# Retention heads on one Trainium2 core: where the first group of new sample states is multiplied

## The reference, cut to what matters

```python
def ret_chunk(state, qkv):
    q, k, v = ...
    decay = jnp.where(diff >= 0, jnp.exp(lg[:, None, None] * jnp.maximum(diff, 0.0)), 0.0)
    qk = jnp.einsum('bihd,bjhd->bhij', q, k) * decay
    o = jnp.einsum('bhij,bjhe->bihe', qk, v)
    o = o + jnp.einsum('bihd,bhde->bihe', q * xi[None, :, :, None], state)
    new_state = (jnp.exp(lg * L)[None, :, None, None] * state
                 + jnp.einsum('bjhd,bjhe->bhde', k * zeta[None, :, :, None], v))
    return new_state, o

def ret_output(o, g, ret_gn, w_out, dtype):
    y = rmsnorm(o, ret_gn.reshape(RET_HEADS, RET_DV)).reshape(b, s, RET_HEADS * RET_DV)
    return ((jax.nn.silu(g.astype(jnp.float32)) * y) @ w_out).astype(dtype)
```

## Time and profile before

| | us |
|---|---|
| median of 3 runs | 1601.35 (1601.34 to 1602.0) |
| profiled execution | 1601.7 |
| its span, first to last instruction | 1599.9 |
| TensorE busy in the span | 1593.4 |
| VectorE busy | 838.5 |
| ScalarE busy | 614.1 |
| POOL busy | 271.3 |

### The profile page before, as it was taken

How to read it: one execution, slowest core, us unless ns; L and a number is a source line. 1 busy time by engine, 2 the same in 40 slices (tenths; PEclk the granted TensorE clock), 3 DMA queues, 4 the chain that set the end, 5 groups by cost and what they waited for, 6 DMA issues and landing times.

```text
span 1599.9 us, 24216 instructions
## 1 busy us (share of the span) xinstructions
PE 1593.4 (100%) x9196; PEld 1536.2 (96%) x9196; DVE 838.5 (52%) x984; ACT 614.1 (38%) x796; POOL 271.3 (17%) x269
## 2 busy tenths in 40 slices
PE   9999999999999999999999999999999999999998
PEld 9999999999999999999999999898989899999987
DVE  6544444787454443445444444674747485444422
ACT  6333222577443332224333223424243354333322
POOL 0111122540211110221111122302030312111000
PEclk9999999999999999999999999999999999999999
DMA  7444344555344443445444345575665755444332
GB/s 219 121 123 131 101 125 142 173 185 171 106 132 127 118 122 109 127 133 140 123 131 123 109 127 191 185 242 207 214 234 190 249 180 141 123 131 131 117 123 102
DMA packets 322145, 239.08 MB, mean 149 GB/s; under 512 B 8432, under 2 KB 286128, under 8 KB 321968
## 3 DMA queue, kind: packets, MB, share of 16 engines
q1 hardware_dynamic: 321808, 237.91, 48.9%
q10 hardware_dynamic: 288, 0.50, 0.1%
HBM read 216.39 MB, written 20.94 MB: 148 GB/s over the span
## 4 chain that ended last, share of the span: by engine, by line
PE 100%; ACT 0%; issue 0%; POOL 0%; DVE 0%; ACTq 0%; POOLq 0%
PE bank L170 26%; PE bank L171 26%; PE bank L172 26%; PE bank L491 2%; PE bank L490 2%; PE bank L489 2%; PE bank L1934 1%; PE bank L1933 1%; PE bank L1932 1%; PE bank L1146 1%; PE bank L398 1%; PE bank L1970 1%; PE bank L2045 1%; PE bank L2001 1%; PE bank L1960 0%; PE bank L985 0%
## 5 line engine op out<-in xcount | busy, mean ns | idle before, releaser
L147 DVE TENSOR_TENSOR WL<-RAW,WH 128x2048 fp32r<-128x2048 f32 (+3 forms) x190 | 399.0, 2102 | 296.0 <-ACT WH L140 295.3
L140 ACT ACTIVATE WH<-RAW 128x2048 fp32r<-128x2048 f32 (+3 forms) x190 | 328.1, 1729 | 560.6 <-PE bank L172 478.1
L170 PE MATMUL bank<-XH,WH 128*128 128x384 f32 x1368 | 458.3, 335 | 0.0
L172 PE MATMUL bank<-XH,WL 128*128 128x384 f32 x1368 | 457.1, 334 | 0.0
L171 PE MATMUL bank<-XL,WH 128*128 128x384 f32 x1368 | 457.0, 334 | 0.0
L170 PEld LDWEIGHTS bank<-XH,WH 128*128 128x128 f32 x1368 | 256.8, 188 | 3.4 <-issue 3.1
L171 PEld LDWEIGHTS bank<-XL,WH 128*128 128x128 f32 x1368 | 256.8, 188 | 0.2
L172 PEld LDWEIGHTS bank<-XH,WL 128*128 128x128 f32 x1368 | 256.8, 188 | 0.0
L655 POOL TENSOR_TENSOR si<-si,rsb 128x384 f32<-128x384 f32 x88 | 94.7, 1076 | 625.3 <-ACT si L526 591.1
L586 DVE TENSOR_TENSOR au<-bank,si 128x384 f32<-128x384 f32 x86 | 48.0, 558 | 250.0 <-PE bank L172 232.3
L170 PE MATMUL bank<-AH,WH 128*128 128x384 f32 x528 | 176.4, 334 | 0.0
(11 more groups left out here) (316 smaller groups left out, 2022.1 us busy)
## 6 DMA issues: line engine op xcount, KB each, us to landing
RAW<-w_ffn_gate_dram SPq DMA_DIRECT2D x86, 512.0 KB, 4.0
RAW<-w_ffn_up_dram SPq DMA_DIRECT2D x86, 512.0 KB, 5.2
RAW<-w_ret_in_dram SPq DMA_DIRECT2D x48, 512.0 KB, 5.1
RAW<-w_ffn_down_dram SPq DMA_DIRECT2D x48, 384.0 KB, 4.0
st<-state_ret_dram SPq DMA_DIRECT2D x32, 512.0 KB, 7.1
new_state_sample_dram<-st SPq DMA_DIRECT2D x32, 512.0 KB, 6.6
RAW<-w_ffn_down_dram SPq DMA_DIRECT2D x48, 320.0 KB, 3.3
RAW<-w_ffn_down_dram SPq DMA_DIRECT2D x22, 512.0 KB, 4.0
```

Source lines behind the costliest of these rows:

```text
L140: ins = act.activation(dst(WH), src, ACT.Copy)
L147: ins = dve.tensor_tensor(dst(WL), src, dst(WH).bitcast(F32), ALU.subtract)
L170: pe.matmul(ps, wh, xh, start=first, stop=False)
L172: return pe.matmul(ps, wl, xh, start=False, stop=last)
```

## The change

It makes four kinds of edits:

- TensorE: group 0 moves from inside gate 1 to directly behind the products of the old states; group 1 moves from gate 2 into gate 1 (ahead of k = 3), group 2 from behind gate 2 into it (ahead of k = 1). Group 0 gets bank 1 in place of bank 5, so `NEW_BANKS` changes for it, the wait for `r_on` goes to group 1, and gate 1, whose bank is 1, waits until group 0 has been taken (`r_ns` 4).
- Pair values: ScalarE writes the sample values twice, straight into `vp`; `vf` and POOL's three copies go. SP starts the four DMAs of each half as soon as that half is written, and from the second head on it issues all eight ahead of the load of chunk 6 instead of behind it (in the first head also ahead of it).
- ScalarE: the high part of the values is written ahead of that of the scores, and ahead of the weight split.
- VectorE: two key rests come ahead of the scores, two behind; values' rest, then scores' rest, then weight split; update 0 directly behind it; then root steps, gate 0, gate 1, update 1.

```diff
-            NEW_BANKS = (bank[2:6] * 3) + [bank[2], bank[3], bank[4], bank[6], bank[7], bank[1]]
+            NEW_BANKS = [bank[2], bank[3], bank[4], bank[1]] + (bank[2:6] * 2) + [bank[2], bank[3], bank[4], bank[6], bank[7], bank[1]]
...
-                    sp.wait_ge(sem("r_vp"), 3 * h + 3)
                     for odd in range(2):
+                        sp.wait_ge(sem("r_vp"), 2 * h + (odd + 1))
                         for j in range(PAIRS):
...
-                            sp.dma_start(vp[other, odd, :], vf[mine, :]).then_inc(sem("r_vd_in"), 16)
+                            sp.dma_start(vp[other, odd, :], vp[mine, odd, :]).then_inc(sem("r_vd_in"), 16)
...
-                    if q == 6:
+                    if q == 5:
                         pair_values(0)
...
+                    pair_values(h)
                     load_weights(h, 6)
-                    pair_values(h)
                     load_weights(h, 7)
...  (pe_head)
+                def new_states(part):
+                    odd, d = part // D, part % D
+                    if part:
+                        pe.wait_ge(sem("r_ns"), N_NEW * h + PAIRS * part)
+                    if part == 3:
+                        pe.wait_ge(sem("r_z"), E * h + 1)
+                    if part == 1:
+                        pe.wait_ge(sem("r_on"), TT * h + 1)
+                    if part == 0:
+                        pe.wait_ge(sem("r_kl"), 4 * h + 4)
+                        pe.wait_ge(sem("r_al"), 2 * h + 1)
...
+                new_states(0)
                 pe.wait_ge(sem("r_vl"), TT * h + TT)
-                pe.wait_ge(sem("r_al"), 2 * h + 1)
+                pe.wait_ge(sem("r_al"), 2 * h + 2)
...
+                    if n == 1:
+                        pe.wait_ge(sem("r_ns"), N_NEW * h + PAIRS)
...
-                gate(1, 3, lambda: new_states(0))
-                gate(2, 1, lambda: new_states(1))
-                new_states(2)
+                gate(1, 3, lambda: new_states(1))
+                gate(2, 1, lambda: new_states(2))
...  (act_head)
-                            act.activation(vf, ps[:, :], ACT.Copy, scale=rsb[:, T + t:T + t + 1]).then_inc(sem("r_v"), 1)
+                            for odd in range(2):
+                                act.activation(vp[:, odd, :], ps[:, :], ACT.Copy, scale=rsb[:, T + t:T + t + 1]).then_inc(sem("r_vp"), 1)
...
+                act.wait_ge(sem("r_vd_in"), self.PAIRED * h + self.PAIRED)
+                act.activation(vd[:, 0, :, :], vp, ACT.Copy).then_inc(sem("r_ah"), 1)
                 act.wait_ge(sem("r_at"), h + 1)
                 act.activation(ah[:, :], at_, ACT.Copy).then_inc(sem("r_ah"), 1)
                 self.look_act(act, h, 3)
-                act.wait_ge(sem("r_vd_in"), self.PAIRED * h + self.PAIRED)
-                act.activation(vd[:, 0, :, :], vp, ACT.Copy).then_inc(sem("r_ah"), 1)
...  (dve_head)
+                key_rests(0)
                 dve.wait_ge(sem("r_scores"), h + 1)
                 dve.tensor_tensor(at_, self.SCORES[:, :], hc[:, DECAY], ALU.mult).then_inc(sem("r_at"), 1)
...
+                key_rests(2)
                 dve.wait_ge(sem("r_ah"), 2 * h + 1)
+                dve.tensor_tensor(vd[:, 1, :, :], vp, vd[:, 0, :, :].bitcast(F32), ALU.subtract).then_inc(sem("r_al"), 1)
+                dve.wait_ge(sem("r_ah"), 2 * h + 2)
                 dve.tensor_tensor(al[:, :], at_, ah[:, :].bitcast(F32), ALU.subtract).then_inc(sem("r_al"), 1)
                 self.look_dve(dve, h, 3)
...
+                new_states(0)
                 dve.wait_ge(sem("r_sq"), TT * h + TT)
...
-                for e in range(2):
-                    gate(e)
-                    new_states(e)
+                gate(0)
+                gate(1)
+                new_states(1)
                 self.look_dve(dve, h, 4)
...  (pool)
-                    pool.tensor_tensor(vp[:, 0, 0:DEC_SEQ], vf[:, 0:DEC_SEQ], ones[:, 0:DEC_SEQ], ALU.mult).then_inc(sem("r_vp"), 1)
-                    pool.tensor_copy(vp[:, 0, DEC_SEQ:HV], vf[:, DEC_SEQ:HV]).then_inc(sem("r_vp"), 1)
-                    pool.tensor_copy(vp[:, 1, :], vf).then_inc(sem("r_vp"), 1)
```

More of the change, by code:

```diff
@@ L1763, in stream_kernel @@
             rst = sb("rst", [P, 3, 4], F32, r)
-            vf = on[:, TT - 1, :]
             vp = sg[:, :, :].rearrange("p e n -> p (e n)")[:, 0:2 * HV].rearrange("p (o n) -> p o n", o=2)
@@ L1971, in pe_head @@
                                       start=(odd == 0 and d == 0), stop=False)
+                def new_states(part):
[9 more added lines that the diff above has]
+                        pe.wait_ge(sem("r_al"), 2 * h + 1)
+                    for n in range(2):
+                        for j in range(PAIRS):
+                            rows = slice(j * PAIR, (j + 1) * PAIR)
+                            mm = pe.matmul(self.NEW_BANKS[PAIRS * part + j][:, :], kl[rows, 2 + odd, d * P:(d + 1) * P],
+                                           vd[rows, n, odd, :], start=(n == 0), stop=(n == 1))
+                    mm.then_inc(sem("r_new"), 1)
+                new_states(0)
                 pe.wait_ge(sem("r_vl"), TT * h + TT)
-                pe.wait_ge(sem("r_al"), 2 * h + 1)
+                pe.wait_ge(sem("r_al"), 2 * h + 2)
                 def weighted(o, block, t, first, last):
@@ L1984, in pe_head @@
                 weighted(o1, 2, 1, False, True).then_inc(sem("r_o"), 1)
[L1988 to L2003, removed]
                 def gate(n, at_k=None, inside=None):
@@ L2199, in dve_head @@
                     ps = self.V_BANKS[t]
-                    dve.wait_ge(sem("r_v"), (TT + 1) * h + (n + 2))
+                    dve.wait_ge(sem("r_v"), TT * h + (n + 1))
                     dve.scalar_tensor_tensor(vl[:, t, :], ps[:, :], rsb[:, T + t:T + t + 1], vh[:, t, :].bitcast(F32),
@@ L2203, in dve_head, with key_rests, new_states @@
                 dve.wait_ge(sem("r_hc_in"), 16 * h + 16)
+                def key_rests(i0):
+                    dve.wait_ge(sem("r_kh"), 4 * h + i0 + 2)
+                    for i in (i0, i0 + 1):
+                        z = ZETA + min(i, 2)
+                        dve.scalar_tensor_tensor(kl[:, i, :], self.turned_keys()[i], hc[:, z:z + 1], kh[:, i, :].bitcast(F32),
+                                                 ALU.mult, ALU.subtract).then_inc(sem("r_kl"), 1)
+                key_rests(0)
                 dve.wait_ge(sem("r_scores"), h + 1)
                 dve.tensor_tensor(at_, self.SCORES[:, :], hc[:, DECAY], ALU.mult).then_inc(sem("r_at"), 1)
[L2206 to L2210, removed]
+                key_rests(2)
                 dve.wait_ge(sem("r_ah"), 2 * h + 1)
+                dve.tensor_tensor(vd[:, 1, :, :], vp, vd[:, 0, :, :].bitcast(F32), ALU.subtract).then_inc(sem("r_al"), 1)
+                dve.wait_ge(sem("r_ah"), 2 * h + 2)
                 dve.tensor_tensor(al[:, :], at_, ah[:, :].bitcast(F32), ALU.subtract).then_inc(sem("r_al"), 1)
                 self.look_dve(dve, h, 3)
-                dve.wait_ge(sem("r_ah"), 2 * h + 2)
-                dve.tensor_tensor(vd[:, 1, :, :], vp, vd[:, 0, :, :].bitcast(F32), ALU.subtract).then_inc(sem("r_al"), 1)
+                def new_states(part):
+                    odd, d = part // D, part % D
+                    dve.wait_ge(sem("r_new"), (4 + D) * h + (part + 1))
+                    for j in range(PAIRS):
+                        n = PAIRS * part + j
+                        old = st[:, 2 * j + odd, d, :]
+                        dve.scalar_tensor_tensor(old, old, hc[:, G16:G16 + 1], self.NEW_BANKS[n][:, :],
+                                                 ALU.mult, ALU.add).then_inc(sem("r_ns"), 1)
+                new_states(0)
                 dve.wait_ge(sem("r_sq"), TT * h + TT)
@@ L2228, in gate @@
                     dve.tensor_tensor(gt[:, e % 2, :], self.G_BANKS[e][:, 0:T], rsb[:, 0:T], ALU.mult).then_inc(sem("r_gt"), 1)
[L2230 to L2237, removed]
                 def z(e):
@@ L2314, in pool @@
                                                        pairs(rot4[:, d, SEQ:T], odd), pairs(rot4[:, 2 + d, SEQ:T], odd), op)                                        .then_inc(sem("r_qz"), 1)
-                    pool.wait_ge(sem("r_v"), (TT + 1) * h + 1)
-                    pool.tensor_tensor(vp[:, 0, 0:DEC_SEQ], vf[:, 0:DEC_SEQ], ones[:, 0:DEC_SEQ], ALU.mult).then_inc(sem("r_vp"), 1)
-                    pool.tensor_copy(vp[:, 0, DEC_SEQ:HV], vf[:, DEC_SEQ:HV]).then_inc(sem("r_vp"), 1)
-                    pool.tensor_copy(vp[:, 1, :], vf).then_inc(sem("r_vp"), 1)
                 norm_adds_pool(pool, self.s + 1)
```

## The result

The changed kernel is slower. Six runs took 1613.97, 1615.48, 1617.08, 1617.10, 1617.21 and 1622.01 us, median 1617.09, against a median of 1601.83 for six runs of the kernel before: a ratio of 1.0097, 95% interval 1.0086 to 1.0108. That is 15.3 us more. The kernel before spreads over 0.7 us, the changed one over 8, and that spread is part of what is to be explained.

What follows compares the result with a forecast made beforehand. The prediction took TensorE's instruction stream to bound the kernel. A new stall of 2.82 us less 0.15 of gaps gave +2.67 us a head, +10.7 over four: 1601.35 + 10.7 = 1612.0 us, range 1610.3 to 1618.9.

Steps and rivals of the forecast that it cites:

- rival A: TensorE's clock falls to half in the stalls: 1618.8 us with four falls, 1613.7 to 1615.4 with one or two; chance 0.26.
- the likeliest case: The forecast itself: four stalls of TensorE, less the gaps saved, clock held; 1612.0 us, chance 0.60.
- Part 4: In gate 2, TensorE's third group waits for VectorE's update 1, held up behind VectorE's gate 1: 2.82 us a head.
- Parts 1 to 3: Gaps around TensorE's tiled groups from moving the first and third: -0.87 + 0.67 + 0.05 = -0.15 us a head.
- parts 1 and 2 alone: First group leaves gate 1 (-0.87 us) and goes behind the old states' products (+0.67): -0.20 us a head.
- The middle value for the switch between two tiled forms: Switch from old states' products to the first group replaces that to the full array: +0.67 us, bounds 0.54 to 0.77.
- the sum: Stall of 2.82 us less 0.15 of gaps: +2.67 us a head, +10.7 over four heads.
- Part 5: Split values reach TensorE's early first group in time, 0.8 us of slack: cost 0, up to 0.3 a head.
- Rival C: Pair DMAs land late, so the first group waits too: 1 to 2 us a head more, 1616 to 1620 us; chance 0.06.
- it is one event: Argument against the clock falling: only one fall seen, at the trace's end, 2.2 us without a matmul; stall hardly longer.
- they may fall all or none: Clock falls would come in all four heads or in none, since the heads are spaced alike.
- Rival B: VectorE's gate 1 runs before TensorE's ends, so no stall and not slower: 1601.2 us; chance 0.04.

Runs made afterwards that it cites:

- experiment 1: Changed kernel with VectorE doing update 1 ahead of gate 1 instead of behind it; 1601.40 us against 1601.55 for the kernel before, ratio 0.9999.
- experiment 2: Changed kernel with TensorE's third group (group 2) back behind gate 2, VectorE's order as changed; 1601.12 us, ratio 0.9997 to the kernel before.
- experiment 7: Kernel before with only VectorE's order changed, to gate 0, gate 1, update 0, update 1; 1623.73 us, ratio 1.0134 to the kernel before.
- experiment 5: As experiment 2, but pair values again written by ScalarE into vf and copied three times by POOL; 1603.07 us against 1601.53 for the kernel before.
- experiment 6: As experiment 2, but SP again loads weight chunk 6 ahead of the pair DMAs; 1602.03 us, ratio 1.0003 to the kernel before.
- experiment 9: Changed kernel with 14 unread matmuls a head ahead of the third group, where TensorE waits for update 1; 1612.43 us against 1601.42 for the kernel before.
- experiment 3: Changed kernel with the third group (group 2) ahead of k = 4 of gate 2 instead of k = 1; 1606.20 us, ratio 1.0030 to the kernel before.
- k = 2: Changed kernel with the third group (group 2) ahead of k = 2 of gate 2 instead of k = 1; 1610.69 us, ratio 1.0056 to the kernel before.
- k = 0: Changed kernel with the third group (group 2) ahead of k = 0 of gate 2 instead of k = 1; 1625.0 us, ratio 1.0148 to the kernel before.

## Why the prediction was right, and where it was short

The prediction gave 1612.0 us, a range of 1610.3 to 1618.9, and 0.94 for slower. The measured median of 1617.09 lies in the range, but where rival A has it, not where the likeliest case does.

- **Part 4, the stall**: right in mechanism and size. With g for the start of the last matmul of gate 1 (1123.67 here), VectorE's gate 1 came at g + 0.38 (predicted 0.37), update 1 at g + 0.85 (0.84), its end at g + 3.56 (3.56), TensorE's restart at g + 3.62 (3.61); the stall is 2.83 (2.82). Experiments 1, 2 and 7 show its cause from three sides.
- **Parts 1 to 3, the gaps**: -0.15 a head predicted, -0.17 measured in experiment 1; parts 1 and 2 alone, -0.20 predicted and -0.20 measured in experiment 2. The first head of the changed kernel, whose clock held, was 85.67 us long against 82.98 before: +2.69, where the sum said +2.67. The middle value for the switch between two tiled forms held: 3.57 us with a tiled group behind as with a full-array matmul. That fits what the Trainium skill says (TensorEngine Tiling (Array Packing), Key Properties), that changing the mode of tiling drains TensorE: here the change from one tiled mode to another took as long as the change to the full array. What a drain costs by itself no run here shows.
- **Part 5, the values in time**: right; no wait of the first group in the trace. The transfers' landing was even quicker, 2.0 us at the median and 2.3 at most, where 2.5 and 4.1 had been read from before. Experiments 5 and 6 show that the cover was real but thin: either of the two edits taken back costs the first head 0.7 to 1.8 us. Rival C's sort of wait exists, then, but not in the changed kernel.
- **Rival A, the clock**: this is the step that failed, "Forecast 0.60, A 0.26". No run of the changed kernel took the 1612.4 us that experiment 9 gives for a full clock; the nearest was 1613.97. The row for it was in the trace of before, a fall 2.2 us behind the last matmul against a stall of 2.8, and it was given too little weight against "it is one event". One event was indeed too few to tell: at the ends of the other ten traces the clock fell 2.7 us (experiment 1) to 4.9 us (experiment 3) behind the last matmul's end, so the distance isn't fixed, and a stall of 2.8 us sometimes brings a fall. Its price, 1.7 us for a fall, was right for one kind of fall and low for the other: the two of the profiled execution cost 4.9 together (1615.4 less 1610.5, the span of experiment 9), 1.6 for the third head's and 3.3 for the fourth's. That "they may fall all or none" is wrong for this execution: two of four heads.
- **Rival B**: it would have needed VectorE's gate 1 to start before TensorE's gate 1 was over. It started 0.38 us behind the last matmul's start, and the time was not 1601.2.

What stays open is why one wait of 2.75 us brings a fall and the next, as long and in the same place, doesn't: the changed kernel had two in four heads, experiment 7 four. How long the clock then stays low does follow a pattern, shown at the end.

## What to carry to other kernels

On an engine that works in order, moving a piece of work earlier moves every wait behind it too. Read the other engine's order against the new one and ask, for each group that waits, which instruction stands in front of its releaser and what that one is waiting for; here it was the very engine that then had to wait. The cost of a stall on TensorE is not its length alone: at 1.2 us it was that within half a microsecond over four heads, at 2.2 us it sometimes was more, and at 2.75 and 3.3 us it cost up to double. If such a wait can't be removed, work of no use in it can be cheaper than standing still, as it was here with 2.75 us (experiment 9).

## What the runs showed of the hardware

Four waits of TensorE, one a head, in a program that otherwise waits only at its start, by their length (wait in each head, time over the kernel before, heads with a fall of the clock in the profiled execution, distance of the lowest to the highest run):

| wait, us | over before, us | falls in 4 heads | runs spread, us |
|---|---|---|---|
| 0.3 (experiment 9, filled) | 11.0 | 0 | 0.5 |
| 1.2 (k = 4) | 4.65 | 0 | 0.8 |
| 2.2 (k = 2) | 9.2 | 1 | 1.7 |
| 2.75 (the change) | 15.3 | 2 | 8.0 |
| 2.75 (experiment 7) | 22.2 | 4 | 5.1 |
| 3.3 (k = 0) | 23.5 | 4 | 2.7 |

The traces of these kernels hold eleven falls in the retention stage, and they are of two kinds, without an exception:

| the clock fell | falls | low for, us | cost, us |
|---|---|---|---|
| 0.2 to 1.6 us behind TensorE's restart | 5 | 3.4 | 1.55 to 1.6 |
| 0.3 to 1.3 us ahead of it, in the wait | 6 | 6.8 | 2.5 to 3.3 |

The cost is what the head was longer than one with the same wait and no fall (for a fourth head, the rest of the span). So the clock stayed low twice as long where it fell while TensorE still stood as where it fell when TensorE had resumed, and the five late falls slowed work that waited for nothing. Experiment 7 cost more than the changed kernel because three of its four falls were long ones. Why the low time has just these two lengths the runs don't show.

At the low level a 384-column matmul follows the last after 0.32 us, 1.85 times 0.173, not twice. The Trainium skill (TensorE: Matmul & The Clock Gate, What's actually happening) gives 2.4 GHz for a busy TensorE and 1.2 GHz for an idle one; the granted 1.00 and 0.50 of these windows are those two levels.
